# Eleven seven-product quads in each column pair, four of them with two sums on GpSimd, and an output stage in another order

## What is computed

```
h = layer_norm(x, emb_ln_g, emb_ln_b)
proj = h @ w_in[l]
q_a, kv_a, dq, dk, dv, g_mla, g_dswa, r_mla, r_dswa = jnp.split(proj, IN_OFFSETS, axis=-1)
a = mla_attention(q_a, kv_a, q_a_norm_g[l], w_q_b[l], kv_a_norm_g[l], w_kv_b[l])
y_mla = (a * jax.nn.silu(g_mla)) @ w_o_mla[l]
b = dilated_mixture(dq, dk, dv, rel_bias)
y_dswa = (b * jax.nn.silu(g_dswa)) @ w_o_dswa[l]
merged = jax.nn.sigmoid(r_mla) * y_mla + jax.nn.sigmoid(r_dswa) * y_dswa
out = merged @ w_out[l]
h = layer_norm(DEEPNORM_ALPHA * h + out, ln_g[l], ln_b[l])
```

## Time and profile before

| | |
|---|---|
| median of 3 runs | 2658.5 us (2655.9 to 2660.7) |
| the profiled execution, its own time | 2661.07 us |
| its span | 2659.3 us |
| PE busy | 2614.8 us, 98% |
| DVE busy | 2219.5 us, 83% |
| ScalarE busy | 1397.1 us, 53% |
| GpSimd busy | 324.0 us, 12% |
| column pairs 0 to 16 | about 188 to 1552 us of the span |
| output pairs | about 2298 to 2541 us |
| "rel" and "fin6" | about 2541 to 2638 us |

### The profile page before, as it was taken

One profiled execution on the slowest core, in us unless ns is written; L12 is line 12 of the kernel. 1 busy time (PEld: TensorE's weight loads), 2 busy tenths in 40 slices (PEclk: granted clock), 3 DMA queues, 4 the chain that ended last, 5 costly groups with the idle time before them and its releaser, 6 DMA issues.

```text
span 2659.3 us, 32135 instructions
## 1 busy us (share of the span) xinstructions
PE 2614.8 (98%) x12174; PEld 2178.7 (82%) x12174; DVE 2219.5 (83%) x2138; ACT 1397.1 (53%) x1306; POOL 324.0 (12%) x444
## 2 busy tenths in 40 slices
PE   7999999999999999999999999999999999999997
PEld 5978888888888888888888889988878888878885
DVE  7779999999999999999999966765575676898868
ACT  5455555555555555665555655544444444455532
POOL 0010111111111111111111101111111100001120
PEclk9999999999999999999999999999999999999998
DMA  6687888888888888888888774466786778878775
GB/s 205 200 296 230 271 263 257 250 244 249 270 262 261 252 241 255 255 270 254 241 249 255 246 229 131 130 187 212 257 258 204 257 231 286 262 216 266 226 250 195
DMA packets 237187, 636.49 MB, mean 239 GB/s; under 512 B 17913, under 2 KB 34661, under 8 KB 236916
## 3 DMA queue, kind: packets, MB, share of 16 engines
q1 hardware_dynamic: 185936, 506.51, 57.2%
q0 software_dynamic: 49888, 125.63, 19.9%
q10 hardware_dynamic: 1224, 2.44, 0.2%
...
## 4 chain that ended last, share of the span: by engine, by line
PE 88%; DVE 5%; DMA 4%; issue 2%; ACT 1%; SPq 0%; DVEq 0%; POOL 0%; ACTq 0%
PE acc L742 9%; PE acc L744 9%; PE acc L743 9%; PE bank L762 4%; PE bank L767 4%; PE bank L766 4%; PE acc L811 3%; PE bank L811 3%; PE acc L762 3%; PE acc L767 3%; PE acc L766 3%; PE acc L815 3%; PE acc L814 3%; PE bank L814 3%; PE bank L815 3%; PE bank L749 3%
## 5 line engine op out<-in xcount | busy, mean ns | idle before, releaser
L1205 ACT ACTIVATE q_hi<-q_raw 128x2048 fp32r<-128x2048 f32 x320 | 613.6, 1918 | 553.6 <-PE bank L751 152.3
L1546 DVE TENSOR_TENSOR q_low<-q_raw,q_hi 128x2048 fp32r<-128x2048 f32 x320 | 729.8, 2286 | 51.4 <-ACT q_hi L1205 49.7
L1445 DVE TENSOR_TENSOR w_lo<-w_raw,w_hi 128x1024 fp32r<-128x1024 f32 (+3 forms) x352 | 387.6, 1115 | 185.5 <-ACT w_hi L1146 179.8
L1146 ACT ACTIVATE w_hi<-w_raw 128x1024 fp32r<-128x1024 f32 (+3 forms) x352 | 329.3, 961 | 158.3 <-PE acc L744 53.4
L1550 DVE TENSOR_TENSOR q_sum_low<-q_sum,q_hi 128x1536 fp32r<-128x1536 f32 x195 | 341.5, 1751 | 0.0
L2170 POOL DMA_DIRECT2D q_raw<-q_raw x195 | 167.3, 858 | 1376.8 <-DMA q_raw<-in_w_in 1181.5
L1208 ACT ACTIVATE q_hi<-q_sum 128x1536 fp32r<-128x1536 f32 x195 | 287.7, 1475 | 60.9 <-DVE q_sum L1538 59.5
L742 PE MATMUL acc<-w_hi,oper_hi 128*128 128x512 f32 (+1 forms) x688 | 261.5, 380 | 4.3 <-DVE w_lo L1445 4.3
L744 PE MATMUL acc<-w_hi,oper_lo 128*128 128x512 f32 (+1 forms) x688 | 256.3, 372 | 0.0
L743 PE MATMUL acc<-w_lo,oper_hi 128*128 128x512 f32 (+1 forms) x688 | 255.8, 372 | 0.0
L1538 DVE TENSOR_TENSOR q_sum<-q_raw,q_sum 128x1024 f32<-128x1024 f32 x195 | 238.9, 1225 | 6.8
(11 more groups left out here) (412 smaller groups left out, 5280.2 us busy)
## 6 DMA issues: line engine op xcount, KB each, us to landing
q_raw<-in_w_in SPq DMA_DIRECT2D x256, 1024.0 KB, 6.8
w_raw<-in_w_in SPq DMA_DIRECT2D x128, 512.0 KB, 4.6
q_raw<-q_raw POOLq DMA_DIRECT2D x195, 256.0 KB, 6.1
...
```

The costliest lines, as they stand in the source:

```text
L1146: act.activation(w_hi[:, n % RING, 0:w], w_raw[:, n % RING, 0:w], ACT.Copy).then_inc(w_hi_ready, 1)
L1205: act.activation(q_hi[h][:, 0:4, :], q_raw[r][:, :, :], ACT.Copy).then_inc(q_hi_ready, 1)
L1445: dve.tensor_tensor(w_lo[:, n % RING, 0:w], w_raw[:, n % RING, 0:w], w_hi[:, n % RING, 0:w].bitcast(F32), ALU.subtract).then_inc(w_lo_read ...
L1546: dve.tensor_tensor(q_low[r], q_raw[r], q_hi[h][:, 0:4, :].bitcast(F32), ALU.subtract).then_inc(q_lo_ready, 1)
```

## The change

`SEVEN` gets quad 13 as its eleventh member, so a T tile more is made in the start stage and the last group of swapped tiles holds two. In pairs 1 to 16 the second and third sums of quads 4, 8, 11 and 13 are made by GpSimd (`other_sums`, two tensor_tensor instructions of 512 and 1024 elements) at positions 4, 8, 12 and 14 of its own queue, behind the first sum of that position; DVE leaves them out, and ScalarE and DVE wait for `pool_sums_ready` instead of `sums_ready`. Pair 0 keeps all sums on DVE. In the output stage, quad 0 of the first output pair takes the second row tile's products first and waits for `m_lo` in finer steps, `last_merged` moves behind quad 1 on PE and behind quad 3 on the others, `last_merge` on DVE behind the low parts of quad 2. The split of the gain and bias rows moves from "fin6" to "rel", and so do the statistics of block 4; the rows of block seven come early in "fin6". On GpSimd the loads for the residual come earlier, and the gain rows are set to zero and loaded ahead of the last pair's adding DMAs. `c_third` of the last pair gets a buffer of its own. Left out below are addresses, declarations and the calls of `third`.

```diff
-SEVEN = (2, 3, 4, 6, 7, 8, 10, 11, 12, 14)
+SEVEN = (2, 3, 4, 6, 7, 8, 10, 11, 12, 13, 14)
 OUT_SEVEN = (2, 4, 5, 7, 8, 10, 11, 13, 14)
-SWAPPED = ((2, 5), (6, 9), (10, 13), (14, 15))
+SWAPPED = ((2, 5), (6, 9), (10, 13), (13, 15))
 SWAP_STEPS = (9, 12, 15)
 STORE_QUAD = 8
+POOL_SUMS = {4: 4, 8: 8, 12: 11, 14: 13}
...
+def pool_sums(g):
+
+    return 0 < g // QUADS < PAIRS and g % QUADS in POOL_SUMS.values()
+
+
+def sums_made_before(g):
+
+    return sum(is_seven(n) and pool_sums(n) == pool_sums(g) for n in range(g))
...
-T_STEPS = (("qa0", 5), ("qa0", 8), ("qa0", 11), ("qa0", 14), ("kva0", 3), ("kva0", 6), ("kva0", 9), ("kva0", 12), ("kva1", 10), ("kva1", 13))
+T_STEPS = tuple(("qa0", j) for j in (5, 8, 11, 14)) + tuple(("kva0", j) for j in (2, 5, 8, 11, 14)) + (("kva1", 10), ("kva1", 13))
 T_MERGE = tuple(f"yd{n + 2}" for n in range(4))
-REL_STATS = (10, 11, 12, 13)
-FIN_STATS = {0: 4, 1: 5}
-FIN_GAINS = {2: 0, 4: 1, 5: 2, 6: 3, 8: 4, 10: 5, 11: 6}
-ROWS_7 = (12, 14)
+REL_HIGH = (4, 5, 6, 7)
+REL_LOW = (5, 6, 7, 8)
+REL_STATS = (9, 10, 11, 12)
+REL_ROWS = (13, 14)
+FIN_GAINS = {4: 0, 5: 1, 6: 2, 7: 3, 8: 4, 9: 5, 10: 6}
+ROWS_7 = (1, 2)
...
+        def third(p):
+
+            return c_last_third if p == LAST_PAIR else c_third
...
-                for i in range(2):
+                for i in (1, 0) if p == PAIRS else (0, 1):
                     for t in range(TT):
+                        if p == PAIRS:
+                            pe.wait_ge(m_lo, KT // 2 - 4 if i else KT // 2 - 3 + t)
...
-                pe.wait_ge(m_lo, KT // 2 - 2)
                 for g in range(NQ, ALL_QUADS):
                     if is_seven(g):
                         seven_quad(g // QUADS, g % QUADS)
                     else:
                         direct_quad(g // QUADS, g % QUADS)
-                    if g == NQ:
+                    if g == NQ + 1:
                         last_merged()
...
-                    act.wait_ge(sums_ready, sevens_before(g) + 1)
+                    act.wait_ge(pool_sums_ready if pool_sums(g) else sums_ready, sums_made_before(g) + 1)
...
-                    if g == NQ + 2:
+                    if g == NQ + 3:
                         last_merged(0)
...
-                elif c.side == "fin6" and j in (6, 8, 10, 12):
-                    cols = slice((j - 6) // 2 * D // 4, ((j - 6) // 2 + 1) * D // 4)
+                elif c.side == "rel" and j in REL_HIGH:
+                    cols = slice(REL_HIGH.index(j) * D // 4, (REL_HIGH.index(j) + 1) * D // 4)
...
             def quad_sums(g):
 
+                if pool_sums(g):
+                    return
...
-                dve.wait_ge(sum_step, m + 1)
+                dve.wait_ge(sum_step, sums_made_before(g) + 1)
...
-                    dve.wait_ge(sums_ready, sevens_before(g) + 1)
+                    dve.wait_ge(pool_sums_ready if pool_sums(g) else sums_ready, sums_made_before(g) + 1)
...
-                last_merge()
...
                     if g == NQ + 2:
+                        last_merge()
+                    if g == NQ + 3:
...
-                elif c.side == "rel" and j in REL_STATS:
-                    row_statistics(REL_STATS.index(j))
-                elif c.side == "rel" and j in (14, 15):
-                    rows_again(6, j - 14)
+                elif c.side == "rel":
+                    if j in REL_LOW:
+                        ln_row_low(REL_LOW.index(j))
+                    if j in REL_STATS:
+                        row_statistics(REL_STATS.index(j))
+                    if j in REL_ROWS:
+                        rows_again(6, REL_ROWS.index(j))
+                    if j == c.slots - 1:
+                        row_statistics(4)
                 elif c.side == "fin6":
...
+            def ln_row_low(n):
+
+                cols = slice(n * D // 4, (n + 1) * D // 4)
+                dve.wait_ge(ln_hi, n + 1)
+                lo = ln_rows_sb[ROWS_LO:ROWS, cols]
+                dve.tensor_tensor(lo, ln_raw[ROWS_LO:ROWS, cols], lo.bitcast(F32), ALU.subtract).then_inc(ln_lo, 1)
...
-                if j in FIN_STATS:
-                    row_statistics(FIN_STATS[j])
+                if j == 0:
+                    row_statistics(5)
+                if j in ROWS_7:
+                    rows_again(7, ROWS_7.index(j))
...
-                if j in (7, 9, 11, 13):
-                    cols = slice((j - 7) // 2 * D // 4, ((j - 7) // 2 + 1) * D // 4)
-                    dve.wait_ge(ln_hi, (j - 5) // 2)
-                    lo = ln_rows_sb[ROWS_LO:ROWS, cols]
-                    dve.tensor_tensor(lo, ln_raw[ROWS_LO:ROWS, cols], lo.bitcast(F32), ALU.subtract).then_inc(ln_lo, 1)
...
+            def other_sums(g):
+
+                r = raw_buffer(g)
+                raw, out_ = q_raw[r], q_sum[sum_buffer(g)]
+                pool.wait_ge(s1_made[r], first_sums(g))
+                pool.wait_ge(quad_done, sum_user_before(g) + 1)
+                steps.done(pool.tensor_tensor(out_[:, 0, :], raw[:, 1, :], raw[:, 0, :], ALU.subtract))
+                steps.wait()
+                s2 = out_[:, 0:1, :].broadcast_to([P, 2, CW])
+                pool.tensor_tensor(out_[:, 1:3, :], raw[:, 3:1:-1, :], s2, ALU.subtract).then_inc(pool_sums_ready, 1)
...
+                if g % QUADS in POOL_SUMS and pool_sums(g - g % QUADS + POOL_SUMS[g % QUADS]):
+                    other_sums(g - g % QUADS + POOL_SUMS[g % QUADS])
...
             slot6 = SEC["out6"].slot0
+            load_resid(0, resid_loaded)
+            load_resid(1, resid_loaded)
+            pool.wait_ge(quad_done, ALL_QUADS)
+            load_last_rows()
             add_pair(LAST_PAIR)
-            for n in range(2 * OUT_PAIRS - 2):
-                pool.wait_ge(slot_done, slot6 + 1 + 2 * n)
+            for n in range(2, 2 * OUT_PAIRS - 2):
+                pool.wait_ge(slot_done, slot6 + 2 * n - 3)
                 load_resid(n, resid_loaded)
+            pool.wait_ge(slot_done, slot6 + 5)
+            load_rows(6)
             pool.wait_ge(fourth_stored, 16 * (LAST_PAIR + 1))
             pool.wait_ge(blocks_stored, 32 * (LAST_PAIR + 1))
-            load_last_rows()
-            pool.wait_ge(slot_done, slot6 + 9)
-            load_rows(6)
             for n in range(2 * OUT_PAIRS - 2, 2 * OUT_PAIRS):
-                pool.wait_ge(slot_done, slot6 + 3 + 2 * n)
+                pool.wait_ge(slot_done, slot6 + 2 * n)
                 load_resid(n, late_resid_loaded)
+            pool.wait_ge(slot_done, slot6 + 12)
+            load_rows(7)
             for n in range(7):
                 pool.wait_ge(slot_done, slot6 + 14 + n)
                 if n >= 2:
                     pool.wait_ge(ln_g_loaded[n % 2], 16 * (n // 2))
                 load_gain(n)
-            load_rows(7)
             pool.wait_ge(ln_g_loaded[1], 48)
             load_gain(7)
 
```

More of the change, by code:

```diff
@@ L376, in program @@
         R_A = RINGS + 48 * K
[L377 removed]
+        R_B = R_A + 43 * K
         R_C = R_B + 16 * K
@@ L407, in program @@
         q_hi = [sb(f"q_hi{n}", at_, [P, 7, CW], F32R) for n, at_ in enumerate((R_C, RINGS, RINGS + 14 * K))]
[L408 to L409 removed]
+        q_sum = [sb(f"q_sum{n}", at_, [P, 3, CW]) for n, at_ in enumerate((SMALL + 3328, SMALL + 3328 + 6 * K, R_A + 37 * K))]
+        q_sum_low = [sb(f"q_sum_low{n}", at_, [P, 3, CW], F32R) for n, at_ in enumerate((SMALL + 3328, SMALL + 3328 + 6 * K, R_A + 37 * K))]
         hx_sb = sb("hx_sb", R_A + 32 * K, [P, TT, CW])
         hx_rows = sb("hx_rows", R_A + 36 * K, [P, 2, CW])
[L412 removed]
+        c_firsts = [sb(f"c_first{n}", R_A + at_ * K, [P, 2, CW]) for n, at_ in enumerate((33, 36))]
         c_third, c_fourth = sb("c_third", R_C + 14 * K, [P, CW]), sb("c_fourth", RINGS + 28 * K, [P, CW])
         c_last = sb("c_last", R_A + 32 * K, [P, CW])
+        c_last_third = sb("c_last_third", R_A + 34 * K, [P, CW])
         qa_hi = sb("qa_hi", R_B, [P, Q_RANK // P, SEQ], F32R)
@@ L525, in program @@
         bias_loaded = [sem(f"bias_loaded{n}") for n in range(2)]
-        (r_sig, merged, mT_ps, m_hi, m_lo, h_done, ln_zeroed, ln_raw_loaded, ln_hi, ln_lo,
+        (r_sig, merged, mT_ps, m_hi, m_lo, h_done, ln_raw_loaded, ln_hi, ln_lo,
          last_ps, last_taken, shift_ready, shift_ps, shift_rows_ready, offsets_ps, y_done, stored) = (
             sem(n) for n in ("r_sig", "merged", "mT_ps", "m_hi", "m_lo", "h_done",
-                             "ln_zeroed", "ln_raw_loaded", "ln_hi", "ln_lo", "last_ps", "last_taken", "shift_ready", "shift_ps",
+                             "ln_raw_loaded", "ln_hi", "ln_lo", "last_ps", "last_taken", "shift_ready", "shift_ps",
                              "shift_rows_ready", "offsets_ps", "y_done", "stored"))
         q_loaded = [sem(f"q_loaded{n}") for n in range(RAWS)]
-        tiles_saved, tiles_back, t1_hi_ready, t1_lo_ready = (
-            sem(n) for n in ("tiles_saved", "tiles_back", "t1_hi_ready", "t1_lo_ready"))
+        tiles_saved, tiles_back, t1_hi_ready, t1_lo_ready, pool_sums_ready = (
```

(9 more changed lines are left out.)

10 lines of the change are left out of this document (4 added, 6 removed).

## The result

The changed kernel takes 2732.2 us (median of 4 runs, 2726.6 to 2733.7) where the kernel before takes 2659.6 (2655.9 to 2661.1): a ratio of 1.0268, 95% interval 1.0255 to 1.0282. It is slower by 72.6 us; 2704 was forecast, in a range of 2642 to 2736.

A forecast was written before the change was run, and what follows sets the result against it. PE bounds the kernel, DVE a near second; with GpSimd's sums DVE becomes the bound. Pairs +49.6, pair 0 -0.7, start +0.4, output stage -3.9 give +45.4, 2706.5 profiled, 2704 as median; range 2642 to 2736.

The forecast's parts named there:

- DVE becomes the bound because GpSimd's reads exclude it: Pairs 1 to 16: GpSimd sums and two-SBUF-input DVE instructions exclude each other; 83.3 us a pair; chance 0.70.
- The price of a set: Pairs: each quad's sums on GpSimd cost DVE 3.3 us, where DVE's own sums cost 1.86.
- GpSimd's sums are hidden: Rival, pairs: sums cost DVE under 8.0 us a pair, PE stays the bound; -15.1, 2643 us; chance 0.17.
- GpSimd starves: Rival, pairs: DVE runs back to back, GpSimd's work comes late; 86 to 88 us a pair, 2747 to 2779; chance 0.08.
- The holds: Pairs: time GpSimd's reads cost DVE, 13.2 us for four quads, less 2.0 covered.
- The cover of quad 4's set: Pairs: quad 4's sums run beside closing adds that read PSUM, so 2.0 us cost DVE nothing.
- DVE's idle time: Pairs: of 4.4 us of DVE's waits for ScalarE in the light quads, 0.6 a pair stay.
- Pairs: Pairs 1 to 16: 83.3 us each, 3.1 more than before, +49.6 in all.
- own work: Pairs 1 to 16: DVE's own work is 71.5 us a pair (75.4 + 3.5 - 7.4).
- Start and pair 0: Start: one more PE wait for the extra T tile, +0.4; pair 0, all sums on DVE, -0.7.
- Output stage: Output stage: rearranged products, merge and closing, together -3.9 us, from -5.9 to +2.2.
- the closing: End of output stage: splits and statistics leave the last chunk, PE's 2.5 us wait for w_lo goes, -2.5.

The follow-up runs named there:

- run 3: Kernel before plus three unused GpSimd tensor_tensor reads of 512 elements at four places in pairs 1 to 16; 2866.2 us, ratio 1.0767.
- run 4: Kernel before plus seven GpSimd memsets of 512 elements, which read nothing, at four places in pairs 1 to 16; 2660.6 us, ratio 1.0002.
- run 1: Changed kernel with all sums back on DVE, nothing else undone; 2663.8 us, ratio 1.0012.
- run 6: Changed kernel with only quad 8's sums on GpSimd; 2677.8 us, ratio 1.0062.
- Run 9: Changed kernel with the sums of quads 4, 8 and 11 on GpSimd, quad 13's on DVE; 2719.3 us, ratio 1.0217.
- run 2: Kernel before with the changed output stage alone, ten seven-product quads, all sums on DVE; 2657.0 us, ratio 0.9981.
- run 7: Changed kernel with all sums on DVE and direct quads at 0, 1, 6, 10, 15, not 0, 1, 5, 9, 15; 2652.2 us, ratio 0.9969.

## Why the prediction was right, and where its sum was off

*DVE becomes the bound because GpSimd's reads exclude it: right, and shown.* Runs 3 and 4 tell reading from being busy and from the queue; run 1 gives back 68 of the 72.6 us. The price of a set, 3.3 us, is what run 6 shows (3.3). The rival "GpSimd's sums are hidden" would have needed q_low at 2.28 us beside a running sum, and no trace shows that. "GpSimd starves" did not come either: the longest of its sums took 3.32 and 4.53 us, 2.0 and 2.1 more than when nothing holds them, less than one q_low; but DVE did keep idle time, as that rival had it.

*The holds: forecast 13.2 - 2.0 = 11.2 us a pair, measured 10.1.* The cover of quad 4's set was mis-sized (1.1 us for 2.0). The holds of all four sets are nevertheless shorter than forecast, because some of the reading falls where DVE stands anyway. The trace of the changed kernel has it: take of each GpSimd sum the last 1.3 or 2.4 us, its own length, as its reading; then 29 us of it, 1.8 a pair, lie beside a standing DVE, nearly all of them with the sums of quad 13, and 13.2 - 1.1 - 1.8 = 10.3.

*DVE's idle time: forecast 0.6 us a pair, measured 3.2. This is the step of the sum that failed.* It was argued that an overloaded DVE hardly waits, and only its waits for ScalarE were counted. Those kept 0.8 us (12.8 / 16); what the sum did not have is waiting for PE. The table, with eleven seven-product quads: 1.2 to 1.9 us with no set or one, 3.2 with three or four. Over half of the 3.2 is one wait, in front of the sums of quad 14 (29.4 of 51.6 us, 9 times). The changed kernel, DVE and then GpSimd:

```profile
748.38 1.75 DVE L1571 TENSOR_TENSOR q_sum_low<-q_sum,q_hi 128x1536 fp32r<-128x1536 f32 x1
753.71 0.69 DVE L1556 TENSOR_TENSOR q_sum<-q_raw 128x512 f32<-128x512 f32 x1 [3.58 <-PE bank L769]
...
749.00 2.28 POOL L2207 TENSOR_TENSOR q_sum<-q_raw 128x512 f32<-128x512 f32 x1 [11.27 <-PE bank L769]
751.36 2.40 POOL L2210 TENSOR_TENSOR q_sum<-q_raw,q_sum 128x1024 f32<-128x1024 f32 x1
```

DVE waits until PE has finished quad 11 and its sum buffer is free, at 753.7. But GpSimd's sums of quad 13, which had waited for quad 10, end at 753.76, and q_low of quad 13 needs them. So two waits end together; each is for one of the three sum buffers, and what a fourth would bring no run shows. From the moment its buffer is free the set takes 4.8 us on GpSimd where DVE takes 1.9, and DVE stands meanwhile.

But this wait is for the most part not lost on top, since GpSimd reads in it and holds nobody. The eight pairs with a wait of 3.6 us there stand for 4.9 us and pay 8.9 of holds, and take 85.1 us; the other eight stand for 1.6, pay 11.6, and take 84.7. So the two terms must be read together: holds and idle time were forecast at 11.2 + 0.6 = 11.8 us a pair and measured at 13.3, and these 1.5 us are nearly all that the pairs came out over the forecast. Run 9, without that set, has as much idle time, in other places (in front of its sums 14.0 us for the adding DMA of the first sum and 16.5 for PE, over the sixteen pairs), and there 2.5 us of GpSimd's reading fall into it: what is shown is that the idle time doesn't go as the load grows, not one single cause for it.

*Pairs: +49.6 forecast, +71.6 measured.* Per pair 84.9 against 83.3: 71.6 own work + 10.1 + 3.2, for 71.5 + 11.2 + 0.6. The pair before is 80.4 on average, where the forecast took 80.2 from one pair.

*TensorE's clock was not in the forecast, and it is hardly in the result.* Twelve of the sixteen pairs contain a stretch at 1.2 GHz (mean clock 0.98) and four don't (1.00). The twelve take 84.9 us on average and the four 84.7. So a pair that waits for DVE hides most of it. PE's busy time has it: 81.5 us a pair, where the forecast had 79 to 80, and in the two windows above 82.1 with such a stretch and 80.5 without.

*Start and pair 0: -0.3 forecast, +4.8 measured.* The T tile in kva0 does bring one more wait, 0.5 to 1.3 us at 133 us in all kernels with five tiles there and in none with four, and PE waits 0.6 to 0.8 us late in pair 0, behind five seven-product quads in a row, which the forecast held to be free. The rest can't be put down to the change with what is measured. PE waits there for the first seven-product quad of all, and the size differs among kernels whose start is the same; the waits of PE from 180 to 200 us, run 4 and then run 3, both with the start of the kernel before:

```profile
PE acc L812 <- DVE q_low L1547: 1.8, 1, 1.8
```

```profile
PE acc L812 <- DVE q_low L1547: 4.6, 1, 4.6
```

It is 1.4 us in the kernel before and 3.9 in the changed one; pair 0 ends at 252.2, 252.7, 253.8 and 257.8 us in the four kernels with ten quads (the last is run 3), and at 254.3 to 259.0 in the nine with eleven.

*Output stage: -3.9 forecast; -3.8 by the sections of the two traces (+0.2, +1.3, -5.4), -5.1 (2.4 to 7.7) in run 2. The sum is right by luck: the closing gained 5.4 us and not 2.5, and the sections before it lost 1.5 where 1.4 were to be won.* The first wait of the output pairs fell from 1.4 us to 0.4, forecast -1.2. In the closing both waits for w_lo have gone, the 1.1 us in "rel" too, which had been put at 0. PE's waits from the last first product to the end, in the changed kernel:

```profile
PE bank L1129 <- DVE shift_cols L2115: 1.9, 1, 1.9
PE acc L1141 <- ACT shift_rows L1450: 0.5, 1, 0.5
PE acc L1141 <- DVE resid L2124: 0.3, 1, 0.3
```

They were there before too. So 3.6 us of waits went, where 2.5 were forecast; the other 1.8 us of the section aren't traced to a wait. The +1.3 holds one PE wait of 1.0 us for q_low that neither run 2 nor run 7 has.

The forecast put +45.4 on the profiled execution and +72.6 came: 22.0 of the difference are the pairs, 5.1 the start, 0.1 the rest. The direction and the mechanism were right, the size was 0.6 of what came, and the range held it by 4 us: in that there is luck, since the holds were put too high and the idle time too low, and the two errors offset each other in part.
